# Hymba block with a hierarchical mixture of experts: routing by token halves, column-wise down weights in whole loads, and an interleaved scatter

## The chip, the core and the metric

The kernel runs on one core of one Trainium2 chip. The metric is the device time of one execution in microseconds (us); lower is better. All data are float32. The five engines are called PE (TensorE), DVE (VectorE), ACT (ScalarE), POOL (GpSimd) and SP (SyncE, which here only issues DMAs).

## What is computed

One block over 256 tokens of width 1024: a mixer (RG-LRU beside causal attention), a cross attention to 256 memory rows, and a mixture of experts, each on a normed input and added to the residual, then a last norm. The change lies at the seam between the cross attention and the experts, and at the end:

```python
h = h + memory_cross_attention(rms_norm(h, norm_cross), mem, ...)      # ends with o @ w_xo
h = h + hier_moe(rms_norm(h, norm_ffn), ...)
return rms_norm(h, norm_final)

# hier_moe, for each token
g_logits = xt @ w_router_group + b_router_group            # 4 groups, the best one is taken
e_logits = xt @ w_router_expert + b_router_expert          # 32 experts, 8 a group, two are taken
gates = g_w * top_p / sum(top_p)
# for each expert, over its tokens
gate, up = split(x @ w_gate_up[e])                         # 1024 x 1024
y = (silu(gate) * up) @ w_down[e]                          # 512 x 1024
out[token] += gate_weight * y
```

All 32 experts are read whatever the routing is: 32 x 6.29 MB (gate/up 4.19 MB, down 2.10 MB).

## The kernel before, in words

The program is one block with an instruction list per engine, ordered by hand; engines meet only at semaphores. PSUM has eight banks; `JOBS` (a table at the top) is the order of their fills, and `begin`, `end`, `release`, `await_fill` and `await_read` turn it into waits. SBUF holds a `ring` of 12 units of 16 KB a partition (2.10 MB each); each of the four experts in flight has three units (`EXPERT_UNITS`): gate/up part 0, gate/up part 1 (contraction rows 0 to 511 and 512 to 1023), and down. Before the experts, parts of the ring serve as landing, split and work buffers of the dense stages.

**Dense stages.** Weights come in 30 halves of 1 MB (`load_half`), are split into a high and a low part by ACT (`split_hi`) and by DVE or POOL (`split_lo`; POOL has halves 6, 8, 10, 12, L1126), and each product is three float32r matmuls (`channels`, L561; `tokens`, L575). A weight half's landing slot and split slot come free at the end of its last use (`LAST_JOB`, `half_used`), and SP's prefetch of expert weights into ring units that are still in use waits for these events (`load_expert`, L442). The last three units of the first four experts wait for half 28 (unit 3), and for the end of job `xo3` (units 4 and 5).

**The seam.** The last projection is four jobs: xo0 and xo1 are columns 0 to 511 of token halves 0 and 1, xo2 and xo3 columns 512 to 1023. DVE adds each to `res` (L1435). PE then transposes `res` (`turn("Tf")`, L544), ACT and DVE copy it with the norm's gain (L899, L1440), PE multiplies by the router (`route`, L758), and `open_sum` (L740) puts `res` into the four accumulator banks with an identity matmul. ACT sums squares (L914), DVE and POOL make 1/rms (L1188, L1120). DVE takes the logits (L1455), finds the best group and two best experts by a chain of small steps (`first_of_max`, L1477 to L1507) for both token halves at once, PE counts ranks (L774 to L776), DVE finds slots (`take_slots`, L1522, L1527), POOL and PE prepare an overflow count. An expert has 32 slots.

**The expert loop.** `Fori` over 8 groups of four experts. PE gathers the group's tokens with one-hot matmuls (L794, 16 matmuls of two records each), DVE writes xg (L1552). For each expert PE does two gate/up parts (L811, 16 matmuls each in four column strips, `gu_used` counts halves of a part), ACT and DVE form silu(gate) * up (L1084, L1562, L1564), PE transposes it (L828), ACT copies it (L899), PE does the down product (L836: 4 k-tiles x 4 strips of 256 columns, strip s holding output columns 256 s to 256 s + 255), and ACT and DVE copy two strips each into `ybuf` (L899, L1568). After the fourth expert PE scatters with four 128x512 matmuls (L845) onto the accumulators. A product of float32 takes two records in the profile. SP refills: gate/up parts at L447 (`load_part`, 16 KB a partition in one load) as `gu_used` allows, down in two loads of 1 MB at L442, each 8 KB a partition, as `y_done` allows.

**The end.** SP loads `norm_final` (0.5 MB, L507) behind the last weights. After the last scatter, for each token half: ACT squares 1024 columns with a sum (L1110), DVE makes the mean (L1188), POOL the power (L1120), DVE scales by it and by the gain (L1613, two of 512 columns), SP stores (L522). Ahead of that every engine loads a flag and branches on it (`value_load`, `If`): the overflow path is not taken.

## Time and profile before

| | |
|---|---|
| device time, median of 3 (lowest, highest) | 672.67 us (672.4, 674.99) |
| the profiled execution: own time, span | 671.75 us, 670.0 us |
| busy: PE, DVE, ACT, POOL | 510.9, 220.9, 168.9, 41.0 us |
| moved by DMA | 237.85 MB, mean 355 GB/s |
| mean granted clock of PE | 0.922 of full |

The span runs from the first to the last recorded event of the execution; the own time also holds what lies around it (1.8 us). All starts below are us from the beginning of the span. A stretch of the granted clock at 1.00 is PE at 2.4 GHz, one at 0.50 is PE at 1.2 GHz. In rows of the timeline, instructions of one line are merged: start, duration from first start to last end, and how many (x); brackets hold the idle time before and what ended it.

### The profile page before, as it was taken

To read this page: it belongs to the slowest core of one execution; us is meant where nothing else is said; L and a number is where in the kernel's file an instruction comes from. 1 tells how busy PE (TensorE), PEld (TensorE's weight loads), DVE (VectorE), ACT (ScalarE), POOL (GpSimd) and SP (SyncE) were. 2 spreads that over 40 slices of the span, in tenths; PEclk is the share of its full clock that TensorE was granted. 3 is DMA by queue.
4 is the path that set the end of the run, shared out by engine and by line. 5 is a ranking of instruction groups with operands and counts; after the bars stand their busy time and mean duration, and the time that the engine had idled before them with its cause. 6 is when DMAs were issued, how large, how long until landed. Compare 5 with 4: busy or idle time off the path is not lost.

```text
span 670.0 us, 11410 instructions
## 1 busy us (share of the span) xinstructions
PE 510.9 (76%) x4768; PEld 351.9 (53%) x4768; DVE 220.9 (33%) x425; ACT 168.9 (25%) x325; POOL 41.0 (6%) x25
## 2 busy tenths in 40 slices
PE   3999999999999987978656756855684585657544
PEld 3988998789888654545223423422352252224221
...
GB/s 345 285 194 183 314 127 142 138 398 248 186 282 382 357 238 425 425 430 427 427 426 427 422 425 426 429 427 426 427 426 424 423 429 427 427 426 427 423 425 156
DMA packets 25637, 237.85 MB, mean 355 GB/s; under 512 B 2832, under 2 KB 2960, under 8 KB 4368
## 3 DMA queue, kind: packets, MB, share of 16 engines
...
q8 instruction: 15, 0.25, 0.1%
q14 instruction: 6, 0.05, 0.0%
HBM read 236.49 MB, written 1.05 MB: 355 GB/s over the span
## 4 chain that ended last, share of the span: by engine, by line
SPq 48%; PE 38%; DMA 7%; issue 3%; DVE 2%; ACT 1%; POOL 1%; DVEq 0%; POOLq 0%
SPq L447 30%; SPq L442 18%; PE psum L575 14%; PE psum L561 11%; DMA ring<-in_w_down 5%; PE psum L811 3%; PE psum L836 2%; DMA landing<-in_dense 1%; PE psum L794 1%; PE psum L544 1%; PE psum L709 1%; PE psum L732 1%; PE psum L845 1%; PE psum L758 1%; POOL stat L1120 1%
## 5 line engine op out<-in xcount | busy, mean ns | idle before, releaser
L811 PE MATMUL psum<-ring,xg 128*32 128x256 f32 x2048 | 152.6, 454 | 87.4 <-DMA ring<-in_w_gate_up 87.4
L811 PEld LDWEIGHTS psum<-ring,xg 128*32 128x32 f32 x2048 | 78.8, 126 | 154.6 <-issue 129.7
L575 PE MATMUL psum<-split_w,split_act 128*128 128x512 f32 x432 | 101.8, 393 | 1.2 <-DVE res L1379 1.2
L575 PEld LDWEIGHTS psum<-split_w,split_act 128*128 128x128 f32 x432 | 80.4, 188 | 18.3 <-DVE res L1379 1.7
L1562 DVE SCALAR_TENSOR_TENSOR small<-small,psum 128x128 f32<-128x128 f32 x32 | 9.2, 288 | 214.8 <-ACT small L1084 214.8
L1084 ACT ACTIVATE small<-psum 128x128 f32<-128x128 f32 x32 | 8.9, 277 | 279.3 <-PE psum L811 279.3
L836 PE MATMUL psum<-ring,small 128*32 128x256 f32 x1024 | 67.2, 400 | 12.9 <-ACT small L899 11.7
L561 PE MATMUL psum<-split_act,split_w 128*128 128x256 f32 x576 | 72.2, 289 | 0.9 <-DVE split_act L1208 0.9
L561 PEld LDWEIGHTS psum<-split_act,split_w 128*128 128x128 f32 x576 | 71.6, 197 | 1.7 <-DVE split_w L1229 1.2
L899 ACT ACTIVATE split_w<-landing 128x2048 fp32r<-128x2048 f32 x30 | 57.4, 1915 | 51.2 <-PE psum L575 27.6
L1195 DVE TENSOR_TENSOR split_w<-landing,split_w 128x2048 fp32r<-128x2048 f32 x25 | 58.9, 2361 | 30.6 <-ACT split_w L899 30.6
L1568 DVE COPY ybuf<-psum 32x256 f32<-32x256 f32 x64 | 27.2, 424 | 95.3 <-PE psum L836 94.8
L836 PEld LDWEIGHTS psum<-ring,small 128*32 128x32 f32 x1024 | 30.2, 113 | 40.0 <-ACT small L899 18.1
L899 ACT ACTIVATE ybuf<-psum 32x256 f32<-32x256 f32 x64 | 23.9, 373 | 72.5 <-PE psum L836 72.2
L1120 POOL TENSOR_TENSOR stat<-stat,ctab 128x2 f32<-128x2 f32 (+2 forms) x7 | 6.9, 991 | 546.6 <-DVE stat L1188 536.6
L845 PE MATMUL psum<-ybuf,small 128*128 128x512 f32 x64 | 29.4, 602 | 8.6 <-DVE ybuf L1568 8.6
L828 PE MATMUL psum<-ctab,small 128*128 128x128 f32 x32 | 10.8, 338 | 30.2 <-DVE small L1564 30.2
L794 PEld LDWEIGHTS psum<-ntake,res 128*128 128x128 f32 x256 | 29.8, 192 | 3.3 <-issue 3.3
L794 PE MATMUL psum<-ntake,res 128*128 128x128 f32 x256 | 29.9, 275 | 0.0
L828 PEld LDWEIGHTS psum<-ctab,small 128*128 128x128 f32 x32 | 4.5, 141 | 47.1 <-DVE small L1564 47.1
L1552 DVE TENSOR_TENSOR xg<-psum,ctab 128x512 f32<-128x512 f32 x16 | 11.1, 691 | 44.5 <-PE psum L794 44.5
L845 PEld LDWEIGHTS psum<-ybuf,small 128*128 128x128 f32 x64 | 11.5, 189 | 23.7 <-ACT ybuf L899 12.3
...
## 6 DMA issues: line engine op xcount, KB each, us to landing
...
```

Of the source, the lines that this page charges most:

```text
L442: sp.dma_start(unit(u)[:, n], src).then_inc(loaded[u][side], 16)
L447: sp.dma_start(unit(u), w_gate_up[e, part]).then_inc(loaded[u][1], 16)
L561: i = mm(b[:, 256 * c:256 * c + 256], w[a][:, k, P * c:P * c + P], src[t][:, k, :], start=k == 0 and n == 0, stop=k == KC - 1 and n == 2)
L575: i = mm(b, src[t][:, k0 + k, P * h:P * h + P], w[a][:, k, :], start=first and k == 0 and n == 0, stop=last and k == CT - 1 and n == 2)
L794: i = mm(bank(GATHER + part)[:, P * k:P * k + P], res[:, h, P * c:P * c + P], ntake[:, h], start=h == 0, stop=h == NH - 1)
L811: i = mm(half[SLOTS * strip:SLOTS * strip + SLOTS], xg[:, CT * part + k, SLOTS * j:SLOTS * j + SLOTS], w[:, k, :, P * strip:P * strip + P] ...
L828: tr(bank(HY)[:, 256:256 + P], hid, ident).then_inc(hid_turned, 1)
L836: i = mm(bank(HY)[SLOTS * strip:SLOTS * strip + SLOTS, 0:256], hidT[:, SLOTS * k:SLOTS * k + SLOTS], w[:, k, 256 * strip:256 * strip + 256 ...
L845: i = mm(bank(ACC_BANKS[2 * h + cb]), give[:, P * h:P * h + P], ybuf[:, 512 * cb:512 * cb + 512], start=False, stop=True, skip_group_check ...
L899: return nc.scalar.activation(dst, src, ACT.Identity, scale=scale, bias=bias)
L1195: V.tensor_tensor(lo, raw(m, chunks_of(m)), hi.bitcast(F32), ALU.subtract).then_inc(w_lo, 1)
L1568: i = V.tensor_copy(ybuf[SLOTS * j:SLOTS * j + SLOTS, 256 * strip:256 * strip + 256], bank(6)[r, 0:256])
```

## The change

- **Routing by token halves.** The last projection does token half 0 over weight halves 28 and 29, then half 0 is turned, routed and chosen, and half 1 of the projection runs behind that; logits, choice, rank and slots are computed for one half at a time (`choose`, `place`, `find_slots`). Squares are summed in four pieces of 512 columns into PSUM. The logits move to another part of `small`.
- **Overflow flag.** It is worked out from the number of tokens of each expert, by two matmuls and three DVE steps ahead of the loop, without POOL.
- **POOL's splits** wait for DVE's convolution (`conv_done`).
- **Down weights** are laid out by output columns (side 0 is 0 to 511, side 1 is 512 to 1023), and loaded as one 2 MB load of 16 KB a partition; for the last expert alone, part 1 and down come in two halves. The down product runs side by side: 2 sides x 4 k-tiles x 4 strips of 128 columns, sides in banks 6 and 4, copied to `ybuf` side by side.
- **Gather** of part 1 is cut: two of four tiles before the first gate/up part, two behind it.
- **Scatter.** Columns 0 to 511 of token half 0 are scattered after side 0 of the fourth expert, the other three behind side 1. The last group is unrolled out of the loop on PE and SP.
- **Norm gain** is loaded after routing into its own buffer (shared with the router's table), ahead of the first refill.
- **Last norm.** Four squares of 512 columns; DVE multiplies by the gain before 1/rms is known, then ACT (columns 0 to 511) and DVE (the rest) scale.

```diff
-    down = np.asarray(inputs["w_down"])[0].reshape(EXPERTS, 2, 2, P, D).transpose(0, 1, 3, 2, 4)
+    down = np.asarray(inputs["w_down"])[0].reshape(EXPERTS, CT, P, 2, 512).transpose(0, 2, 3, 1, 4)
     return {"in_w_gate_up": np.ascontiguousarray(gate_up).reshape(EXPERTS, 2, P, UNIT),
-            "in_w_down": np.ascontiguousarray(down).reshape(EXPERTS, 2, P, HALF)}
+            "in_w_down": np.ascontiguousarray(down).reshape(EXPERTS, P, UNIT)}
...
-        latetab = sb("latetab", [P, (KC + 1) * N_ROUTES])
+        after_routing = sb("after_routing", [P, D])
+        latetab = after_routing[:, 0:(KC + 1) * N_ROUTES]
...
-                    src = w_gate_up[e, part, :, n] if part < 2 else w_down[e, side]
+                    src = (w_gate_up[e, part] if part < 2 else w_down[e])[:, n]
                     sp.dma_start(unit(u)[:, n], src).then_inc(loaded[u][side], 16)
 
             def load_part(e, j, part):
 
                 u = EXPERT_UNITS[j][part]
-                sp.dma_start(unit(u), w_gate_up[e, part]).then_inc(loaded[u][1], 16)
+                src = w_gate_up[e, part] if part < 2 else w_down[e]
+                sp.dma_start(unit(u), src).then_inc(loaded[u][1], 16)
...
+            for h in range(NH):
+                await_read(sp, f"route{h}")
+            sp.dma_start(gain_final, norm_final.partition_broadcast(P)).then_inc(gain_loaded, 16)
+            def refill(g, last):
+
                 for j in range(BATCH):
                     for part in range(2):
                         sp.wait_ge(gu_used, 4 * BATCH * g + (4 * (j - BATCH) + 2 * part + 2))
-                        load_part(BATCH * g + j, j, part)
-                    sp.wait_ge(y_done, BATCH * g + (j + 1 - BATCH))
-                    load_expert(BATCH * g + j, j, 2)
-            sp.wait_ge(gu_used, 4 * (EXPERTS - BATCH + 1))
-            sp.dma_start(gain_final, norm_final.partition_broadcast(P)).then_inc(gain_loaded, 16)
+                        if last and j == BATCH - 1 and part:
+                            load_expert(BATCH * g + j, j, part)
+                        else:
+                            load_part(BATCH * g + j, j, part)
+                    if last and j == BATCH - 1:
+                        for side in range(2):
+                            sp.wait_ge(y_done, 2 * BATCH * g + (2 * (j - BATCH) + side + 1))
+                            load_expert(BATCH * g + j, j, 2, (side,))
+                    else:
+                        sp.wait_ge(y_done, 2 * BATCH * g + (2 * (j - BATCH) + 2))
+                        load_part(BATCH * g + j, j, 2)
+
+            with sp.Fori(1, BATCHES - 1) as g:
+                refill(g, False)
+            refill(BATCHES - 1, True)
...
             tokens_whole(26, ["xo0", "xo1"], ys_, "xpv")
-            tokens(28, ["xo2", "xo3"], ys_, 0, last=False)
+            tokens(28, ["xo2", "xo3"], ys_, 0, last=False, halves=(0,))
+            tokens(29, ["xo2", "xo3"], ys_, CT, first=False, halves=(0,))
             for c in (0, 1):
                 await_read(pe, f"xo{c}")
             turn("Tf", res, (0, 1))
-            tokens(29, ["xo2", "xo3"], ys_, CT, first=False)
-
-
...
             pe.wait_ge(router_loaded, 16)
-            route(0)
-            for c in (2, 3):
-                await_read(pe, f"xo{c}")
-            turn("Tf", res, (2, 3))
-            route(1)
-            open_sum(0)
-
+            for c in (0, 1):
+                await_read(pe, f"Tf{c}")
+            route(0, 0)
+            route(1, 0)
+            await_read(pe, "Tf2")
+            route(0, 1)
+            tokens(28, ["xo2", "xo3"], ys_, 0, last=False, halves=(1,))
+            tokens(29, ["xo2", "xo3"], ys_, CT, first=False, halves=(1,))
+
+            picked = rt(4)
             pe.wait_ge(chosen, 1)
-            picked = rt(4)
-            b = begin("rank")
-            mm(b[:, 0:EXPERTS], const("before"), picked[:, 0], start=True, stop=True)
-            mm(b[:, EXPERTS:2 * EXPERTS], const("before"), picked[:, 1], start=True, stop=False)
-            end(mm(b[:, EXPERTS:2 * EXPERTS], ones, picked[:, 0], start=False, stop=True), "rank")
-            open_sum(1)
+            end(mm(begin("rank0")[:, 0:EXPERTS], const("before"), picked[:, 0], start=True, stop=True), "rank0")
+            open_sum(0, 0)
+            await_read(pe, "xo3")
+            turn_late("Tf3", 1, (4, 5))
+            turn_late("Tf4", 1, (6, 7))
+            open_sum(1, 0)
+            for c in (3, 4):
+                await_read(pe, f"Tf{c}")
+            route(1, 1)
+            begin("rank1")
+            mm(pb("rank1")[:, 0:EXPERTS], ones, picked[:, 0], start=True, stop=False)
+            pe.wait_ge(late_sumsq, 2 * NH)
+            open_sum(0, 1)
+            open_sum(1, 1)
+            pe.wait_ge(chosen, 2)
+            end(mm(pb("rank1")[:, 0:EXPERTS], const("before"), picked[:, 1], start=False, stop=True), "rank1")
             GATHER, HY, GU = 4, 6, 7
             for h in range(NH):
                 await_read(pe, f"route{h}")
-            await_read(pe, "rank")
-
-            pe.wait_ge(over_ready, 1)
+                await_read(pe, f"rank{h}")
+            picked_all = rt(4)
             begin("over")
-            end(mm(pb("over")[:, OVER:OVER + NH * EXPERTS], ones, rt(12).rearrange("p h e -> p (h e)"), start=True,
-                   stop=True), "over")
-            with pe.Fori(0, BATCHES) as g:
+            for h in range(NH):
+                i = mm(pb("over")[:, OVER:OVER + EXPERTS], ones, picked_all[:, h], start=h == 0, stop=h == NH - 1)
+            end(i, "over")
...
+            def scatter(g, cb, halves):
+
+                pe.wait_ge(y_act, 2 * BATCH * g + (2 * BATCH + cb - 1))
+                pe.wait_ge(y_dve, 2 * BATCH * g + (2 * BATCH + cb - 1))
+                for h in halves:
+                    mm(bank(ACC_BANKS[2 * h + cb]), give[:, P * h:P * h + P], ybuf[:, 512 * cb:512 * cb + 512],
+                       start=False, stop=True, skip_group_check=True).then_inc(scattered, 1)
+
+            def group(g, last):
+
 
                 pe.wait_ge(taken, g + 1)
-                for part in range(2):
-                    for k in range(CT):
+                def gather(part, ks):
+
+                    for k in ks:
                         for h in range(NH):
                             c = CT * part + k
                             i = mm(bank(GATHER + part)[:, P * k:P * k + P], res[:, h, P * c:P * c + P],
                                    ntake[:, h], start=h == 0, stop=h == NH - 1)
-                    i.then_inc(gathered, 1)
+                    if ks[-1] == CT - 1:
+                        i.then_inc(gathered, 1)
+
+                gather(0, range(CT))
+                gather(1, range(2))
...
+                            if part:
+                                gather(1, range(2, CT))
                             pe.wait_ge(xg_ready, 2 * g + (1 + part))
...
+                    for side in range(2):
+                        if last and j == BATCH - 1:
+                            pe.wait_ge(loaded[u][side], (32, 16 * BATCHES)[side])
+                        elif side == 0:
+                            pe.wait_ge(loaded[u][0], 16)
+                            pe.wait_ge(loaded[u][1], 16 * g + 16)
+                        for k in range(CT):
+                            for strip in range(BATCH):
+                                i = mm(bank((HY, GATHER)[side])[SLOTS * strip:SLOTS * strip + SLOTS, 0:P],
+                                       hidT[:, SLOTS * k:SLOTS * k + SLOTS], w[:, side, k, P * strip:P * strip + P],
+                                       start=k == 0, stop=k == CT - 1, tile_position=(0, SLOTS * strip))
+                        i.then_inc(y_done, 1)
+                        if j == BATCH - 1:
+                            scatter(g, 0, (side,))
+                scatter(g, 1, range(NH))
+
+            with pe.Fori(0, BATCHES - 1) as g:
+                group(g, False)
+            group(BATCHES - 1, True)
...
+            late_squares(0, 0)
             turned_tokens(0)
-            for h in range(NH):
-                await_read(act, f"xo{2 + h}")
-                sum_squares(res, 4, (h,))
-            turned_tokens(2)
-            act.wait_ge(group_arg, 1)
+            late_squares(1, 0)
+            late_squares(0, 1)
+            late_squares(1, 1)
...
-            for h in range(NH):
-                act.wait_ge(scattered, NH * (BATCHES - 1) + h + 1)
-                nc.scalar.activation(final_squares.rearrange("p (c n) -> p c n", c=2), psum[:, 2 * h:2 * h + 2, :], ACT.Square,
-                                     accum_out=stat[:, SS + FINAL + h:SS + FINAL + h + 1]).then_inc(final_sq, 1)
-                act.wait_ge(final_sq, h + 1)
+            for cb in range(2):
+                for h in range(NH):
+                    act.wait_ge(scattered, 2 * NH * (BATCHES - 1) + 2 * cb + h + 1)
+                    col = SS + FINAL + 2 * cb + h
+                    nc.scalar.activation(final_squares[:, 0:512], bank(ACC_BANKS[2 * h + cb]), ACT.Square,
+                                         accum_out=stat[:, col:col + 1]).then_inc(final_sq, 1)
+                    act.wait_ge(final_sq, 2 * cb + h + 1)
+            for h in range(NH):
+                act.wait_ge(final_gain, h + 1)
+                act.wait_ge(final_rstd, h + 1)
+                copy(fin[:, h, 0:512], fin[:, h, 0:512], stat[:, RS + FINAL + h:RS + FINAL + h + 1]).then_inc(final_act, 1)
...
+            pool.wait_ge(conv_done, 1)
             split_lo(6)
...
+            for h in range(NH):
+                pool.wait_ge(meansq, 4 + h)
+                power(6 + h, 1, rstd)
...
+            choose(0)
+            add_xo("xo3", 1, 1)
+            late_tokens("Tf4", 6, 2, 1)
+            late_mean(1)
+            place(0)
+            link(find_slots(0, 0))
+            slots_times_rstd(0)
+            choose(1)
+            place(1)
+            find_slots(1, 0).then_inc(slots_found, 1)
+            dve.wait_ge(slots_found, 1)
+            slots_times_rstd(1).then_inc(taken, 1)
...
+            await_fill(dve, "over")
+            link(V.tensor_reduce(soft[:, 0:1], pb("over")[:, OVER:OVER + EXPERTS], AX.X, ALU.max))
+            link(V.tensor_scalar(soft[:, 0:1], soft[:, 0:1], SLOTS + 0.5, None, ALU.is_ge))
+            release(V.tensor_copy(flag, soft[:, 0:1]), "over")
+            await_read(dve, "over")
...
+            def times_gain(h, cb):
+                n = slice(512 * cb, 512 * cb + 512)
+                return V.tensor_tensor(fin[:, h, n], bank(ACC_BANKS[2 * h + cb]), gain_final[:, n], ALU.mult)
+
             for h in range(NH):
                 dve.wait_ge(final_sq, h + 1)
-                mean(FINAL + h, 1, D).then_inc(final_ms, 1)
+                times_gain(h, 0).then_inc(final_gain, 1)
+            link(mean(FINAL, NH, D))
+            for h in range(NH):
+                dve.wait_ge(final_sq, 3 + h)
+                col = MS + FINAL + h
+                V.scalar_tensor_tensor(stat[:, col:col + 1], stat[:, SS + FINAL + 2 + h:SS + FINAL + 3 + h], 1.0 / D,
+                                       stat[:, col:col + 1], ALU.mult, ALU.add).then_inc(final_ms, 1)
+                times_gain(h, 1).then_inc(final_gain, 1)
+            for h in range(NH):
+                dve.wait_ge(final_gain, NH + h + 1)
                 dve.wait_ge(final_rstd, h + 1)
-                for cb in range(2):
-                    n = slice(512 * cb, 512 * cb + 512)
-                    V.scalar_tensor_tensor(fin[:, h, n], bank(ACC_BANKS[2 * h + cb]),
-                                           stat[:, RS + FINAL + h:RS + FINAL + h + 1], gain_final[:, n],
-                                           ALU.mult, ALU.mult).then_inc(final_out, 1)
+                V.tensor_scalar(fin[:, h, 512:], fin[:, h, 512:], stat[:, RS + FINAL + h:RS + FINAL + h + 1], None,
+                                ALU.mult).then_inc(final_dve, 1)
...
```

## Rows read from the trace of the kernel before

**Rows 1.** The page, 40 slices of 16.75 us: GB/s moved by DMA

```profile
GB/s 345 285 194 183 314 127 142 138 398 248 186 282 382 357 238 425 425 430 427 427 426 427 422 425 426 429 427 426 427 426 424 423 429 427 427 426 427 423 425 156
```

**Rows 2.** The page, chain that ended last, share of the span by engine

```profile
SPq 48%; PE 38%; DMA 7%; issue 3%; DVE 2%; ACT 1%; POOL 1%; DVEq 0%; POOLq 0%
```

**Rows 3.** Windows: us, busy of PE, PEld, DVE, ACT, POOL, granted clock, DMA share, GB/s

```profile
233.00:241.00 8.00, 8.00 (x94) 6.04 (x96) 5.17 (x21) 0.00 (x0) 0.47 (x1) 1.00 0.10 39
241.00:243.00 2.00, 1.33 (x19) 0.53 (x11) 0.57 (x2) 0.66 (x2) 0.00 (x0) 1.00 0.92 221
...
250.00:640.00 390.00, 262.66 (x3107) 141.22 (x3107) 60.01 (x170) 40.09 (x122) 0.00 (x0) 0.88 1.01 426
224.00:231.00 7.00, 6.89 (x20) 4.59 (x20) 3.23 (x21) 0.21 (x1) 0.70 (x1) 0.51 1.00 378
```

**Rows 4.** Timeline of SP's DMA issues before the expert stream

```profile
214.12 0.80 SPq L442 DMA_DIRECT2D ring<-in_w_gate_up  x2
...
220.47 0.80 SPq L442 DMA_DIRECT2D ring<-in_w_gate_up  x2
...
240.24 2.05 SPq L447 DMA_DIRECT2D ring<-in_w_gate_up  x2
```

**Rows 5.** Timeline of PE at the seam

```profile
214.72 5.72 PE L575 MATMUL psum<-split_w,split_act 128*128 128x512 f32 x24
...
220.28 1.87 PE L758 MATMUL psum<-latetab,xg 128*128 128x36 f32 x16
...
224.11 3.60 PE L758 MATMUL psum<-latetab,ybuf 128*128 128x36 f32 x16 [1.06 <-DVE ybuf L1440]
...
234.32 3.65 PEld L794 LDWEIGHTS psum<-ntake,res 128*128 128x128 f32 x32
```

**Rows 6.** Timeline of DVE at the seam

```profile
220.48 0.69 DVE L1435 TENSOR_TENSOR res<-psum,res 128x512 f32<-128x512 f32 x1 [2.03 <-PE psum L575]
...
228.12 0.29 DVE L1477 TENSOR_REDUCE soft<-small 128x8 f32<-128x64 f32 x2
...
231.44 0.22 DVE L1507 TENSOR_TENSOR small<-small 128x64 f32<-128x64 f32 x1
...
233.74 0.48 DVE L1527 TENSOR_SCALAR ntake<-small,stat 128x128 f32<-128x128 f32 x2
...
236.52 0.68 DVE L1552 TENSOR_TENSOR xg<-psum,ctab 128x512 f32<-128x512 f32 x1
```

**Rows 7.** Timeline of PE in the last group, gate/up products released by landings

```profile
623.36 3.62 PE L811 MATMUL psum<-ring,xg 128*32 128x256 f32 x32 [2.97 <-DMA ring<-in_w_gate_up]
...
633.23 3.26 PE L811 MATMUL psum<-ring,xg 128*32 128x256 f32 x32 [2.60 <-DMA ring<-in_w_gate_up]
638.13 1.93 PE L811 MATMUL psum<-ring,xg 128*32 128x256 f32 x32 [1.65 <-DMA ring<-in_w_gate_up]
```

**Rows 8.** Timeline of the end of the span (and one down product of an earlier expert)

```profile
628.70 1.93 PE L836 MATMUL psum<-ring,small 128*32 128x256 f32 x32 [0.37 <-ACT small L899]
...
657.75 0.59 PEld L836 LDWEIGHTS psum<-ring,small 128*32 128x32 f32 x16 [0.61 <-DMA ring<-in_w_down]
658.89 0.76 ACT L899 ACTIVATE ybuf<-psum 32x256 f32<-32x256 f32 x2 [2.40 <-PE psum L836]
...
659.91 3.67 PE L845 MATMUL psum<-ybuf,small 128*128 128x512 f32 x8 [1.08 <-DVE ybuf L1568]
...
663.68 1.02 ACT L1110 ACTIVATE ring<-psum 128x1024 f32<-128x1024 f32 x1 [0.66 <-PE psum L845]
...
664.60 0.19 ACT L1110 ACTIVATION_READ_ACCUMULATOR ring<-psum 128x1 f32 x1
...
666.10 1.41 DVE L1613 SCALAR_TENSOR_TENSOR ring<-psum,stat,ring 128x512 f32<-128x512 f32 x2 [0.67 <-POOL stat L1120]
```

**Rows 9.** Timeline of DVE's convolution and POOL's first split behind it

```profile
36.71 5.09 DVE L1273 SCALAR_TENSOR_TENSOR work<-work,ctab 128x256 f32<-128x256 f32 x12
...
43.00 5.49 POOL L1126 TENSOR_TENSOR split_w<-landing,split_w 128x2048 fp32r<-128x2048 f32 x1 [18.53 <-ACT split_w L899]
```

252 lines of the change are left out of this document (134 added, 118 removed).

## The prediction

> **What bounds the kernel now.** I read the page's slices first. From slice 15 on the DMA engines move 422 to 430 GB/s in every slice until the last one, while before it they are often half idle [rows 1]. The chain of waits says the same: 48% of the span is the DMA queue's own issuing, which stands blocked behind transfers in flight [rows 2]. The windows by stage then give the sizes: 426 GB/s at a DMA share of 1.01 over the 390 us from 250 to 640, with PE busy two thirds of that time, DVE 60 us and ACT 40 us [rows 3]. So the expert stage is a stream of bytes: 28 experts x 6.29 MB remain to be loaded after the ring of four experts is full, 176 MB at 426 GB/s = 413 us, and nothing that compute does within it matters. The time is: when that stream starts, its rate, and what follows its last byte.
>
> **Its start.** The windows show 39 GB/s in 233 to 241: the ring is full and nothing may be loaded until the first expert's first half of gate/up weights has been used. That is the issue at 240.24 [rows 4]; with the thin 241 to 243 (221 GB/s) behind it [rows 3] the stream has an effective start of 242.0 (0.44 MB by 243). The path to 240.24 by engine: PE's last output projection ends near 220.44, DVE adds xo3 at 220.48, the route parts follow, then 3.5 us of choosing (228.12 to 231.66, both token halves together), the gather from 234.38 and half a gate/up product behind it [rows 5, 6]. Within it the granted clock fell to 0.5 of full (0.51 over 224 to 231 [rows 3]), and as many records of routing took 3.60 us instead of 1.87 [rows 5].
>
> **Its end.** The last half of down weights lands at 657.75, the span ends at 669.96: a tail of 12.2 us [rows 8].
>
> **The change part by part.** All times are on the scale of the profiled execution (span 669.96, own time 671.75, which is 0.9 below the median of 672.67).
>
> *GpSimd's split behind the convolution.* The added wait is for DVE's convolution, whose last operations run from 36.71 for 5.09 us, to 41.80; GpSimd's first such split starts at 43.00 today, released by ACT [rows 9]. The wait is met before it is reached: 0. What queues behind it on GpSimd starts no later.
>
> *Routing by halves.* PE now does token half 0 of the last projection first (24 of the 48 matmuls), then turns and routes half 0, then does half 1. 24 of its matmuls take 5.6 us (5.72 for a stretch with its hand-over [rows 5]). Half 0 is done at 213.9, the turns (8+4 transposes of 128x128, 0.12 each) by 215.5, the three route parts (24 records at 0.117 [rows 5], after DVE's copies) by about 218.9, half 1 (24 matmuls) by 224.4: xo3 comes 3.9 us later than today. Choosing one half lies between 1.8 us (half of 3.54) and 3.5; most of a step is fixed cost, so I take 3.2. For half 0 it lies under the half-1 matmuls and costs nothing; uncovered it would cost those 3.2 us. After 224.4 on the path: rank0 0.3, open_sum 0.92 (four matmuls of 512 columns in 3.67 [rows 8]), turns 0.5, open_sum 0.92, route 0.95, some 0.4 of hand-overs = 228.4; logits and 3.2 us of choosing, to 232.0; rank, place and slots of one half 1.5, to 233.5. So the slots are there 0.7 us before today's 234.22 (233.74 + 0.48 [rows 6]), although two choices are now made instead of one.
>
> *Gather split, overflow flag ahead of the loop.* Only 24 of 32 gather records (0.115 each [rows 5]) stand ahead of the first gate/up half, so PE could begin at 236.4. But DVE's xg is late next: today it ends at 237.20, 3.0 us after the slots (gates, gtake, xg [rows 6]), and the flag's three new steps with their waits, 0.25 each, go in between. xg: 233.5 + 3.0 + 0.75 = 237.3; product 1.93 [rows 7]; first refill issued at 239.4 instead of 240.24. **Gain 0.8**, which would be 1.5 without the flag. The flag's matmuls lie in PE's wait: 0.
>
> *What that hands to the queue.* SP's loads of the last three prefetch units hang on the projection: one at 214.12 (after weight half 28), two from 220.47 (after xo3) [rows 4]. In the new order half 28 is free only after its second use, at 221.7, and xo3 at 224.5. Counted back from 233.5, the last two units ran from 222.4 (9.8 us and 1.3 lost) and the one before from about 216.3 or 216.5, so the load before that ends near 216.3. There the queue now runs dry; it idles to about 223.2, then needs 3 x 4.9 = 14.7 us, to 238 or 239, where now it was done at 233.5. The norm gain, 0.5 MB or 1.2 us, is moved from behind the last weights, where it was free, to just there. So the queue comes dry at 239 to 240, right when the first refill is issued. The idle time is moved, not removed: 8 us of it lay at 233 to 242, now 7 lie at 216 to 223. An even faster route would bring little. Effective start 241.2 instead of 242.0: **-0.8**, between -2.5 (queue never dry again) and +5 (rival C).
>
> *Down weights in 2 MB loads.* A row of a partition becomes 16 KB instead of 8. The matmuls that wait for landings give the price: from gate/up part 1 of one expert to part 0 of the next (a down unit in halves and a gate/up unit) 623.36 to 633.23 = 9.87, then one gate/up unit 633.23 to 638.13 = 4.90 [rows 7]. Down costs 4.97 where gate/up costs 4.90. For the 27 units still to come that are merged: 27 x 0.07 = 1.9; the last expert's part 1 is now split (+0.1), and an unrolled last group means more instructions to fetch (+0.1). **-1.7**, between 0 (the differences are one hundredth of a reading) and -2.7 (0.1 each). What the loads' own start costs is weighed under rival D.
>
> *Narrow down products.* 16 matmuls of 256 columns become 32 of 128: 32 records in 1.93 us [rows 8] become 64. If streaming stays the limit it is still 1.9 us; if each record keeps its 0.06 us, 3.9. I take 1.9: four strips run side by side and 128x128 records come at 0.114 each when alone. Either way PE waits for weights in the stream (it is busy two thirds of it), so the price there is 0; in the tail it is 0 to 1.8.
>
> *Tail.* Today, after 657.75 (16 of the down product's 32 records are left, 1.0 us): copies to 659.7, four scatter matmuls 3.67, square and read-out until 664.8, mean and power to 666.10, two products of 0.7, the store from 667.5 to 669.96 [rows 8]. New: columns 0 to 511 are done and scattered for half 0 before the last megabyte lands (that scatter ends at about 658.1, 0.4 late; if that overlap fails it is the 0.92 of the matmul); side 1 takes 0.9, copies 0.6 (0.76 at twice the width), ACT's load of the flag 0.5 (its price is not shown: it lies today between 659.7 and the first square, two squares of 1.02 and their gap before 664.8, so 0 to 2.2; I take the low part, being one word), four squares of about 0.87 (half of 1.02, read-out 0.19, hand-over) to 663.8, where ACT and no longer PE's 2.8 us of scatter ends last. Power until 665.1, DVE's last gain product and two scalings (0.7 + 2 x 0.4) to 666.1 instead of 667.5. **-1.4**, between -2.5 and +0.5.
>
> Sum: -0.8 - 1.7 - 1.4 = **-3.9**: own time 667.9, and against the median 672.67 - 3.9 = **668.8**.
>
> **The rivals.** About 0.5% (3.4 us) is what a measurement of this kernel can tell from no change.
>
> *B, the clock falls under the early route.* From 213.9 to 218.9 PE now does only transposes, 36-column products and waits, as it does today from 220.4 to 224.1, after which the clock was 0.51 over 224 to 231. Then part of half 1's matmuls run at half speed: the rows price it at 1.7 (3.60 - 1.87), more if longer; xo3 moves to 226.3 or later, first refill to 241.1, effective start 242.9: the first term becomes +0.9 and the time 670.5. For it: the stretch is as thin and longer than today's. Against: dense matmuls follow at once. Chance 0.33. The Trainium skill's page TensorE: Matmul & The Clock Gate, section HAM oscillation, says that PE waiting between bursts falls back to the low clock; the trace's clock row agrees.
>
> *C, slower: the clock is low from xo3 through the first group.* While half 1 is chosen PE has nothing (about 230.4 to 232.1) and then only small products. If the clock is at half from 224.4 on, route and sums add 3.0, the gather 2.7, the first gate/up product 1.3 (3.26 against 1.93 [rows 7]): from an issue at 239.4 to one at 246.4 at most; part of the gather lies beside DVE's 0.9, so 245.5. The stream starts at 247 instead of 242, +5.0 - 3.1 = +1.9: 674.6. It decides once the low clock covers the gather; without that it is rival B. Chance 0.06.
>
> *D, every load has a start of its own.* After the idle stretch the first bytes came about 1.1 us after the issue at 240.24 [rows 3, 4]. If each of the 27 merged loads saved that, 30 us would go: 638. Against it stands 426 GB/s at share 1.01 with halves and whole loads mixed in the queue: the start is hidden in the queue. Chance 0.01. The Trainium skill's page DMA: Bandwidth & Descriptors, section Bandwidth, gives 341 GB/s for single 1 MB transfers and 425 for 16 MB and asks for large ones; by its figures merging would bring about 1.3 us each, an estimate of 36 us. The trace disagrees for loads that are queued.
>
> *E, the change does not do what it says in the tail.* Narrow products at 0.06 a record and ACT's flag load late: the tail brings 0, 670.2. Chance 0.12.
>
> **How the numbers follow.** Forecast case 0.48, 665.6 to 670.0 by its own bounds; B 0.33, E 0.12, C 0.06, D 0.01. Faster by over 0.5% (below 669.3) is four fifths of the forecast case, a third of B, a quarter of E and D: 0.53. Slower by over 0.5%: 0.05 (C where the packets bring nothing as well, and B where the low clock lasts). Within: 0.42. The range, 665.2 to 671.9, holds the forecast case and most of B and E.
>
> **What would show it.** Right: DMA near zero at 217 to 223 and almost none at 235 to 240; xo3's add near 224.6; issue of the first refill near 239.4; landings 4.90 apart for all three units of an expert; last landing to end of span about 10.8. Wrong: a gap in the DMA just before the first refill, PEclk 0.5 after 216 or in the gather, a rate that stays 426, or a tail of 12. I would be most wrong if the late prefetch loads push the stream's start past 242.

## The result, and the profile after

Changed kernel 666.59 us (665.56 to 669.61, 6 runs), kernel before 672.6 us (671.19 to 678.04, 6 runs) on the same chip: ratio 0.989, 95% interval [0.9858, 0.9922]. The number came out inside the range that was predicted (668.8, range 665.2 to 671.9), and faster by over 0.5%, which was given 0.53. A later measurement of the same kernel (e6, 12 runs, below) gave 0.9939 [0.9908, 0.9969]. Medians and ranges here are of all executions, while the ratios leave out those over 1.5% above the fastest of their kernel: one of e4's, and four of the kernel before beside e1 to e8. The profiled execution has a span of 664.3 and a time of its own of 666.09, where before had 669.96 and 671.75: 5.7 us less.

The page of the changed kernel, slices and chain by engine (against [rows 1, 2]), and its loads of whole units (kind and count, KB each, median us from issue to landing):

```profile
GB/s 357 283 199 177 318 135 178 131 403 230 190 279 356 296 374 428 431 427 427 427 427 431 427 431 427 428 427 427 430 428 431 428 427 427 427 431 429 427 419 148
...
PE 44%; DMA 38%; SPq 11%; DVE 3%; ACT 1%; issue 1%; POOL 1%; ACTq 0%; DVEq 0%
...
ring<-in_w_gate_up SPq DMA_DIRECT2D x55, 2048.0 KB, 49.3
ring<-in_w_down SPq DMA_DIRECT2D x27, 2048.0 KB, 49.4
```

Its windows, columns as in rows 3:

```profile
216.00:223.00 7.00, 7.00 (x34) 5.37 (x34) 3.78 (x22) 0.20 (x1) 0.00 (x0) 1.00 0.38 128
232.00:235.00 3.00, 3.00 (x18) 2.78 (x21) 1.61 (x7) 0.00 (x0) 0.00 (x0) 0.50 1.02 423
233.00:239.00 6.00, 5.22 (x54) 3.69 (x56) 2.04 (x6) 0.00 (x0) 0.00 (x0) 0.82 0.89 322
250.00:640.00 390.00, 270.57 (x4063) 172.41 (x4057) 69.70 (x230) 49.72 (x181) 0.00 (x0) 0.87 1.01 428
```

And its timeline, from the first product to the stores:

```profile
13.62 11.87 PE L579 MATMUL psum<-split_act,split_w 128*128 128x256 f32 x96 [0.86 <-DVE split_act L1287]
...
36.02 5.09 DVE L1352 SCALAR_TENSOR_TENSOR work<-work,ctab 128x256 f32<-128x256 f32 x12
...
41.19 6.61 POOL L1205 TENSOR_TENSOR split_w<-landing,split_w 128x2048 fp32r<-128x2048 f32 x1 [17.40 <-DVE work L1352]
...
206.07 0.69 DVE L1513 TENSOR_TENSOR res<-psum,res 128x512 f32<-128x512 f32 x1 [0.53 <-PE psum L593]
...
230.50 4.43 PE L839 MATMUL psum<-ntake,res 128*128 128x128 f32 x24
...
237.11 4.13 SPq L453 DMA_DIRECT2D ring<-in_w_gate_up  x2
...
628.61 1.93 PE L865 MATMUL psum<-ring,xg 128*32 128x256 f32 x32 [1.69 <-DMA ring<-in_w_gate_up]
633.50 2.76 PE L865 MATMUL psum<-ring,xg 128*32 128x256 f32 x32 [2.95 <-DMA ring<-in_w_gate_up]
...
638.39 3.34 PE L894 MATMUL psum<-ring,small 128*32 128x128 f32 x64 [0.58 <-DMA ring<-in_w_down]
...
643.29 1.93 PE L865 MATMUL psum<-ring,xg 128*32 128x256 f32 x32 [1.56 <-DMA ring<-in_w_gate_up]
...
648.18 1.07 PE L865 MATMUL psum<-ring,xg 128*32 128x256 f32 x16 [1.42 <-DMA ring<-in_w_gate_up]
...
651.05 1.08 PE L894 MATMUL psum<-ring,small 128*32 128x128 f32 x32 [0.37 <-ACT small L956]
...
652.94 1.10 PE L827 MATMUL psum<-ybuf,small 128*128 128x512 f32 x2 [0.81 <-DVE ybuf L1691]
653.97 1.08 PE L894 MATMUL psum<-ring,small 128*32 128x128 f32 x32
654.98 2.84 PE L827 MATMUL psum<-ybuf,small 128*128 128x512 f32 x6
...
659.84 1.81 SPq L540 DMA_DIRECT2D out<-ring  x4
```

What to see. The queue runs dry at 216 to 223 (128 GB/s) and is busy at 233 to 239 (322 GB/s), the reverse of [rows 3]: the idle time was moved, as forecast. Landings, read from the products that they release, are 4.89 to 4.90 apart for all three units of an expert (628.61, 633.50, 638.39, 643.29), where down took 4.97. But the largest piece lies where I had put zero: the add of xo1, which comes ahead of everything that the change does to the routing, is at 206.07 instead of 208.68. Cut at three points, the 5.7 us are: start to that add -2.61; add to first refill 31.04 instead of 31.56, -0.52; first refill to the last gate/up landing 411.07 instead of 412.65 (652.89 - 240.24 in the trace of before), -1.58; that landing to the end 16.12 instead of 17.07, -0.95.

### The profile page after: what moved, and what is told of

Same layout as the page of the kernel before. It is cut to its first block, busy times and chain, and to the rows that moved or that the text cites. A ratio compares the mean times of both kernels' runs of the same rounds, so it can differ in the third digit from the quotient of the medians.

```text
span 664.3 us, 13610 instructions
## 1 busy us (share of the span) xinstructions
PE 515.4 (78%) x5794; PEld 381.9 (57%) x5794; DVE 236.3 (36%) x518; ACT 181.3 (27%) x399; POOL 42.0 (6%) x25
## 4 chain that ended last, share of the span: by engine, by line
PE 44%; DMA 38%; SPq 11%; DVE 3%; ACT 1%; issue 1%; POOL 1%; ACTq 0%; DVEq 0%
DMA ring<-in_w_gate_up 29%; PE psum L593 15%; SPq L453 11%; PE psum L579 10%; DMA ring<-in_w_down 8%; PE psum L865 6%; PE psum L894 3%; PE psum L839 2%; PE psum L827 2%; DMA landing<-in_dense 1%; PE psum L750 1%; PE psum L727 1%; PE psum L562 1%; SPq L447 1%; PE psum L771 1%
## 5 line engine op out<-in xcount | busy, mean ns | idle before, releaser
L865 PE MATMUL psum<-ring,xg 128*32 128x256 f32 x2048 | 139.6, 420 | 66.0 <-DMA ring<-in_w_gate_up 59.7
L865 PEld LDWEIGHTS psum<-ring,xg 128*32 128x32 f32 x2048 | 73.5, 118 | 119.1 <-issue 82.5
L894 PE MATMUL psum<-ring,small 128*32 128x128 f32 x2048 | 80.7, 319 | 23.7 <-DMA ring<-in_w_down 16.0
L894 PEld LDWEIGHTS psum<-ring,small 128*32 128x32 f32 x2048 | 67.6, 128 | 40.3 <-issue 26.8
L1691 DVE COPY ybuf<-psum 32x128 f32<-32x128 f32 x128 | 37.2, 291 | 121.9 <-PE psum L894 121.1
L956 ACT ACTIVATE ybuf<-psum 32x128 f32<-32x128 f32 x128 | 34.2, 267 | 99.0 <-PE psum L894 98.3
L1199 POOL TENSOR_TENSOR stat<-stat,ctab 128x1 f32<-128x1 f32 (+2 forms) x8 | 7.3, 912 | 550.7 <-DVE stat L1737 433.6
L827 PE MATMUL psum<-ybuf,small 128*128 128x512 f32 x64 | 37.0, 704 | 6.5 <-DVE ybuf L1691 6.5
L839 PE MATMUL psum<-ntake,res 128*128 128x128 f32 x256 | 33.6, 287 | 0.1
L1205 POOL TENSOR_TENSOR split_w<-landing,split_w 128x2048 fp32r<-128x2048 f32 x4 | 21.4, 5338 | 30.6 <-DVE work L1352 17.4
```

The lines of the kernel that those rows point to most:

```text
L827: mm(bank(ACC_BANKS[2 * h + cb]), give[:, P * h:P * h + P], ybuf[:, 512 * cb:512 * cb + 512], start=False, stop=True, skip_group_check=Tru ...
L839: i = mm(bank(GATHER + part)[:, P * k:P * k + P], res[:, h, P * c:P * c + P], ntake[:, h], start=h == 0, stop=h == NH - 1)
L865: i = mm(half[SLOTS * strip:SLOTS * strip + SLOTS], xg[:, CT * part + k, SLOTS * j:SLOTS * j + SLOTS], w[:, k, :, P * strip:P * strip + P] ...
L894: i = mm(bank((HY, GATHER)[side])[SLOTS * strip:SLOTS * strip + SLOTS, 0:P], hidT[:, SLOTS * k:SLOTS * k + SLOTS], w[:, side, k, P * strip ...
L956: return nc.scalar.activation(dst, src, ACT.Identity, scale=scale, bias=bias)
L1205: nc.gpsimd.tensor_tensor(lo, raw(m, chunks_of(m)), hi.bitcast(F32), ALU.subtract).then_inc(w_lo_pool, 1)
```

## The experiments

The same cuts for every profiled execution (us). "First product" and "convolution" are the durations of the lines of 13.62 and 36.02 above. "To first refill" is from xo1's add to the issue of the first refill, "to last gate/up landing" from there to the start of the product that the last gate/up weights release (in e11 and e12, where idle products stand before it, to the landing itself), and "to end" from there to the end of the span.

| kernel | first product | convolution | xo1 add at | to first refill | to last gate/up landing | to end | span |
|---|---|---|---|---|---|---|---|
| before | 13.93 | 5.09 | 208.68 | 31.56 | 412.65 | 17.1 | 670.0 |
| after | 11.87 | 5.09 | 206.07 | 31.04 | 411.07 | 16.1 | 664.3 |
| e1 before again | 11.87 | 9.42 | 213.07 | 29.91 | 412.54 | 19.5 | 675.0 |
| e2 before, whole down | 13.44 | 5.09 | 207.72 | 33.27 | 410.53 | 19.4 | 670.9 |
| e3 after, half down | 13.25 | 5.09 | 207.91 | 31.09 | 412.4 | 16.8 | 668.2 |
| e4 after, no wait | 11.86 | 9.48 | 212.31 | 35.48 | 410.43 | 16.2 | 674.4 |
| e5 before, wait | 11.88 | 5.09 | 206.38 | 29.91 | 412.56 | 17.1 | 665.9 |
| e6 after again | 13.2 | 5.09 | 207.89 | 31.08 | 410.29 | 18.6 | 667.9 |
| e7 after, old seam | 13.52 | 5.09 | 207.43 | 30.94 | 410.52 | 19.7 | 668.6 |
| e8 after, scatters late | 13.91 | 5.09 | 208.69 | 31.05 | 410.54 | 17.0 | 667.3 |
| e9 before, wait, whole down | 11.88 | 5.09 | 206.12 | 31.58 | 410.37 | 18.2 | 666.3 |
| e10 after, gather filled | 11.89 | 5.09 | 207.05 | 32.61 | 410.46 | 17.7 | 667.8 |
| e11 after, tail filled | 13.74 | 5.1 | 208.15 | 31.07 | 410.4 | 16.5 | 666.1 |
| e12 after, both filled, scatters and gain late | 13.22 | 5.09 | 207.45 | 31.02 | 410.6 | 16.8 | 665.9 |

### e1, e4, e5: GpSimd's wait

e1 is the kernel before, unchanged, beside e2 to e4. e4 takes the wait out of the changed kernel, e5 puts it, and nothing else, into the kernel before:

```diff
 e4
-            pool.wait_ge(conv_done, 1)
             split_lo(6)
 ...
 e5
+            pool.wait_ge(conv_done, 1)
             split_lo(6)
 ...
```

> The kernel before, unchanged, for a second profile of it. Theory A (the start of the span differs by chance): the first product of 96 matmuls, 13.93 us in the profile of before and 11.87 in that of after, takes another value here, anywhere from 11.8 to 14, according to when the granted clock rises, so that the seam may start up to 2.6 us earlier without any change. Rival B (the change itself made the start quicker): it is again close to 13.9, and the end of job xo1 again near 208.7. Both: last landing to end of span 12.2 us, rate 426 GB/s, ratio 1.00.

> The changed kernel without GpSimd's wait for the convolution. My step said that the wait costs and brings nothing, as it is met before it is reached. In the profile of after the split starts at 41.19 on the wait's release, 1.0 us after ACT had its part ready. Theory A: gain and loss within 0.2 us at the end of the first gate product and at xo1. Rival B (GpSimd beside the convolution slows DVE, and the wait brings the 2 us of the start): convolution's last 12 steps take over 5.5 us instead of 5.09, and xo1 ends 2 us later.

> The kernel before with one line more: GpSimd waits for the end of the convolution ahead of its first split of weights in that stage; nothing else of the change. Theory (the stalled step): where TensorE's clock rises early, so that the first product takes 11.87 us, the split of the kernel before begins at about 40.6 us beside the convolution, and one step of VectorE stands for 4.8 us; with the wait the convolution takes 5.1 us in every execution, the split begins at 41.2 at the earliest, and about half of the executions get 3 to 4.5 us shorter. The median falls by 1.5 to 3.5 us (ratio 0.995 to 0.998), the slowest executions fall to about 674 and the fastest stay as they are. Rival (the wait is worth nothing, as I predicted, and the early stages of the changed kernel were shorter by the clock's chance alone): ratio 1.000 within 0.002, with the same spread of 671 to 682, and a convolution of over 9 us in a profile whose first product takes 11.87.

Measured: e1 675.33 us (670.96 to 678.88), ratio 0.9995 [0.9963, 1.0027]. e4 672.48 (667.62 to 678.13), 0.9948 [0.9912, 0.9984]. e5 669.89 (667.37 to 675.39), 0.9929 [0.9896, 0.9961], beside a before of 673.5. One line of the change, alone, makes the kernel 3.6 us faster by the medians (2.6 to 7.0 by the interval of the ratio): nearly as much as the whole change beside it (e6, 669.67). Taking the line out of the changed kernel shows less clearly what it is worth: e4's ratio of 0.9948 stands against 0.989 and 0.9939 with the line, and the intervals overlap.

The timelines show how. The first product in the profile of before, and then e1, where it is shorter:

```profile
14.30 13.93 PE L561 MATMUL psum<-split_act,split_w 128*128 128x256 f32 x96 [0.88 <-DVE split_act L1208]
```

```profile
13.92 11.87 PE L561 MATMUL psum<-split_act,split_w 128*128 128x256 f32 x96 [1.27 <-DVE split_act L1208]
...
36.31 9.42 DVE L1273 SCALAR_TENSOR_TENSOR work<-work,ctab 128x256 f32<-128x256 f32 x12
...
40.55 4.89 POOL L1126 TENSOR_TENSOR split_w<-landing,split_w 128x2048 fp32r<-128x2048 f32 x1 [16.46 <-ACT split_w L899]
...
47.99 2.50 PE L575 MATMUL psum<-split_w,split_act 128*128 128x512 f32 x5 [4.09 <-DVE split_w L1195]
```

The convolution's twelve steps in e1 (durations in ns, minimum, median, maximum; first and last start):

```profile
L1273 DVE SCALAR_TENSOR_TENSOR work<-work,ctab x12: 480/481/4808, 36.3 to 40.9; 128x256 f32<-128x256 f32 x12
```

Eleven steps take 0.48 us; one, beside GpSimd's split of 4.89 us, takes 4.81. PE then waits 4.1 us for DVE's own split behind it, and the add of xo1 comes at 213.07. Whether the two meet hangs on the first product. Where it takes 11.87, ACT is ready with its part at 40.5 to 40.8 and lets GpSimd go while DVE still convolves, which would last until 41.4 to 41.6. Where it takes 13.2 to 13.9, that hand-over comes at 41.8 to 43.0, behind the convolution, as in [rows 9] and e2, which have no wait either. e5 with a short first product:

```profile
36.39 5.09 DVE L1274 SCALAR_TENSOR_TENSOR work<-work,ctab 128x256 f32<-128x256 f32 x12
...
41.56 6.61 POOL L1126 TENSOR_TENSOR split_w<-landing,split_w 128x2048 fp32r<-128x2048 f32 x1 [17.39 <-DVE work L1274]
...
206.38 0.69 DVE L1436 TENSOR_TENSOR res<-psum,res 128x512 f32<-128x512 f32 x1 [0.54 <-PE psum L575]
...
236.29 2.06 SPq L447 DMA_DIRECT2D ring<-in_w_gate_up  x2
```

Among the short starts the two without the wait (e1, e4) add xo1 at 213.07 and 212.31, the four with it (after, e5, e9, e10) at 206.07 to 207.05: 6 to 7 us each time. The long starts lie at 207.4 to 208.7 with or without it. So in these profiles the wait doesn't give 6 us to all executions; it turns the worst case into the best one. Six of fourteen profiles had the short start; 6/14 of 6.5 us is 2.8, an estimate near the 3.6.

The Trainium skill, page SBUF — State Buffer, section Who interferes with whom, says that a VectorE instruction with two inputs in SBUF contends with a GpSimd instruction that reads SBUF, and that the loser is blocked for the whole of the other's instruction. The trace agrees: 4.81 us beside 4.89, in place of 0.48. The other way round fits too: above, GpSimd's split at 41.19 takes 6.61, where others take 4.58 to 4.60. DVE's split (41.03, 2.29 us) came first and ended at 43.32, and from there to the end of GpSimd's at 47.80 are 4.48 us; there nobody waits for it.

Why the first product has two lengths isn't settled. In the windows from 14 to 20, before got through 29 of its records and e1 through 50 (0.20 and 0.12 us each), while the column of the granted clock stands at 1.00 in both.

### e2, e3: the down weights' rows

e2 gives the kernel before 16 KB rows and one 2 MB load per down unit; e3 takes the merging back in the changed kernel's loop:

```diff
 e2 (np.asarray(inputs["w_down"])[0] is left out of the first two lines)
-    down = ....reshape(EXPERTS, 2, 2, P, D).transpose(0, 1, 3, 2, 4)
+    down = ....reshape(EXPERTS, CT, P, D).transpose(0, 2, 1, 3)
...
-                    load_expert(BATCH * g + j, j, 2)
+                    load_part(BATCH * g + j, j, 2)
...
 e3
-                        load_part(BATCH * g + j, j, 2)
+                        load_expert(BATCH * g + j, j, 2)
...
```

> The kernel before with down weights in rows of 16 KB and one 2 MB load for each refill, nothing else. If bytes in packets of 8 KB are slower by the 0.07 us for 2 MB that the landings showed: 28 x 0.07 = 1.9 us off the stream, 428 GB/s instead of 426 in 250 to 640, landings 4.90 apart, span about 668 where nothing else differs, ratio 0.997. Rival (the 2 MB loads bring nothing, the gain is the seam and the tail): rate stays at 426, ratio 1.000. Rival (each load has a start of its own): 30 us less.

> The changed kernel with the down refills in two loads of 1 MB of 8 KB rows again (the columns stay by sides, the product waits for each side alone). If the rows of 16 KB are what made the stream faster: rate back to 426 in 250 to 640, down units 4.97 instead of 4.90, span longer by 1.8 to 2.6 us. Rival (the rate came from fewer waits of the queue, not from packets): rate stays 428.

Measured: e2 672.65 us (669.31 to 678.08), 0.997 [0.9934, 1.0006]; e3 670.11 (668.57 to 672.77), 0.9931 [0.9904, 0.9957]. The medians alone don't settle 2 us in a kernel that spreads over 8. The stream does: first refill to last gate/up landing is 412.4 to 412.7 in the four executions with 8 KB rows (before, e1, e3, e5) and 410.3 to 411.1 in the ten others of the table, whatever else they do. The rate from 250 to 640 is 426 GB/s with the halves and 428 or 429 without. Merging is worth 2.0 us of the stream. e3's landing is read from this row of weight loads, since its products ran on at the low clock past it:

```profile
651.41 0.45 PEld L865 LDWEIGHTS psum<-ring,xg 128*32 128x32 f32 x8 [0.41 <-DMA ring<-in_w_gate_up]
```

What in the merging does it isn't separated: both runs change the length of the rows and the number of loads together. By their pages e2 moved the same bytes as before in 21605 packets instead of 25637, which is 144 fewer for each of the 28 merged pairs, and 16 of these 144 are packets under 512 bytes (2384 in all instead of 2832).

### e6, e7, e8: routing by halves, and the scatter between the sides

e6 is the changed kernel again. e7 gives it back the routing of both halves together. e8 moves the scatter:

```diff
 e8
                         i.then_inc(y_done, 1)
-                        if j == BATCH - 1:
-                            scatter(g, 0, (side,))
+                scatter(g, 0, range(NH))
                 scatter(g, 1, range(NH))
```

> The changed kernel unchanged, as the measure for the two runs beside it. If the stalled step explains its narrow spread: 665.5 to 670, median 666.5 to 668.5, and a profile with a convolution of 5.1 us. If that was luck of its six executions: some at 671 or over, and a convolution of over 9 us where the first product takes 11.87.

> The changed kernel with the routing of before: both token halves together (adds, turns, logits, choice, ranks, slots), all else of the change kept, the slots of the gather ahead of the loop among it. Theory: the split of the gather stays, so the first refill is issued about 0.5 us later than in the changed kernel measured from the add that opens the stage (31.5 in place of 31.0), and the kernel is 0.3 to 0.8 us slower than the changed kernel in the same job. Rival (the halves gain more than that, since they keep TensorE busy through the routing and so hold its clock up): the windows of the route show 0.5 to 0.8 of the clock and the kernel is 1.5 us or more slower. Rival (the halves bring nothing): the same within 0.2 us.

> The changed kernel with all four scatter products of the last two experts behind both sides of the last down product, as one block, in place of one scatter between the sides. In the changed kernel's trace the product of side 1 (653.97) waited 1.0 us behind a scatter that waited for its rows, with its weights long there. Theory: side 1 follows side 0 at once and ends 0.75 to 1.0 us earlier, its copies with it, and the last scatter, which then carries one product more (0.55 us), ends 0.2 to 0.7 us earlier; last landing to end shrinks by that, and the kernel is 0.2 to 0.7 us faster than the changed kernel. Rival (the change's own reason, that the early scatter takes work off the end): 0.3 to 0.6 us slower, since one scatter of 0.55 to 0.6 us comes behind the last copy.

Measured: e6 669.67 us (667.75 to 671.67), 0.9939 [0.9908, 0.9969]; e7 670.95 (665.03 to 672.98), 0.9938 [0.9905, 0.9972]; e8 668.31 (666.67 to 669.05, 6 runs), 0.9901 [0.9862, 0.9939]. e6 lies 1 to 2 us above my expectation, and three of its runs are at 671 or over (671.08, 671.3, 671.67), which I had named as the sign that the first six executions were low by luck; its profile had a long first product, so it doesn't test the stalled step. e7's ratio is e6's, though its median is 1.3 us higher and its runs spread over 8 us, where e6's spread over 4. The table shows e7's first refill no later (30.94) than with the halves (31.04 to 31.09). So the theory's 0.5 us isn't seen, but intervals of 0.3% either way can't exclude it. e6, its timeline and two windows:

```profile
232.32 4.57 PE L839 MATMUL psum<-ntake,res 128*128 128x128 f32 x24
...
238.97 4.14 SPq L453 DMA_DIRECT2D ring<-in_w_gate_up  x2
...
649.26 1.07 PE L865 MATMUL psum<-ring,xg 128*32 128x256 f32 x16 [1.42 <-DMA ring<-in_w_gate_up]
...
652.20 1.79 PE L894 MATMUL psum<-ring,small 128*32 128x128 f32 x32 [0.43 <-ACT small L956]
...
656.74 1.94 PE L894 MATMUL psum<-ring,small 128*32 128x128 f32 x32
```

```profile
232.00:235.00 3.00, 2.94 (x16) 2.83 (x16) 2.35 (x14) 0.00 (x0) 0.00 (x0) 0.60 1.03 434
653.00:659.00 6.00, 5.21 (x55) 2.80 (x48) 0.84 (x3) 0.78 (x3) 0.00 (x0) 0.50 0.04 15
```

Two things are to be read here. The gather of 24 records takes 4.57 us, with the granted clock at 0.50 for a part of it. That is so in all of after, e3, e6, e8 and e11 (4.43 to 4.58, mean granted clock 0.62 to 0.64 over the gather). In the kernel before 32 records took 3.79 in four profiles of five (before, e1, e5, e9, at 1.00; 4.64 in e2), and with the old routing in the changed kernel (e7) 24 took 2.92, at 1.00. And in the tail the clock is at the 1.2 GHz level in e6 and e7, and the down products of 32 records take 1.8 to 1.9 us each; in after and e4 it is at 2.4 and they take 1.08. Between landing and end these profiles are 2.5 to 3.6 us apart (16.1 against 18.6 and 19.7).

e8, whose clock was low for part of the tail:

```profile
650.28 1.56 PE L865 MATMUL psum<-ring,xg 128*32 128x256 f32 x16 [1.42 <-DMA ring<-in_w_gate_up]
...
653.76 3.64 PE L894 MATMUL psum<-ring,small 128*32 128x128 f32 x64 [0.37 <-ACT small L955]
...
657.33 3.79 PE L827 MATMUL psum<-ybuf,small 128*128 128x512 f32 x8
```

It ended 17.0 us after the landing, 1.6 sooner than e6. With both sides in one block there is no second wait for copies (0.81 in the timeline of after) and no scatter at half speed ahead of the last weights' product. That the scatter between the sides, which the change added for the tail, costs time where the clock is low is an argument from these two profiles, and the clock came back at different times in them; the intervals of e6 and e8 overlap. Where the clock is high, e12 ends its scatters no sooner than after.

### e9: two parts of the change alone

The kernel before with the edits of e2 and e5.

> The kernel before with two parts of the change alone: GpSimd's wait behind the convolution, and the down weights in one 2 MB load of 16 KB rows each. No routing by halves, no split gather, no narrow down products, no scatter between the sides, gain still last in the queue. Theory (the wait is worth 2 to 3.6 us in the median, the rows 2.0 us of stream, and the rest of the change next to nothing on average): ratio 0.989 to 0.993, level with the whole change; from the first refill's issue to the last gate/up landing 410.5 us in place of 412.6. Rival (the rest of the change brings 1.5 us or more, by slots, split gather and tail, as I predicted 2.2 of it): ratio 0.994 or above, and over 1.5 us behind the changed kernel (0.989 and 0.994 in its two measurements).

Measured: 669.95 us (667.0 to 675.7), 0.9941 [0.9907, 0.9974], beside a before of 674.84. By the ratio it falls to the rival by a hair; the interval holds both. It is level with the changed kernel's second measurement and 0.005 behind its first. Its stream is as expected, 410.37. Nine of its twelve runs lie between 667.0 and 670.6 and three between 674.8 and 675.7, a group that e6's twelve runs don't have; no profile fell in it, so its cause is open.

### e10, e11, e12: keeping TensorE busy

e10 runs three products of 512 columns, read by nobody, ahead of the wait for the second choice; e11 runs such products in the last expert's waits; e12 is both, with e8's scatters and the gain vector's load moved behind the last weights.

```diff
 e10
+            for _ in range(3):
+                mm(bank(4), ident, res[:, 0, 0:512], start=True, stop=True, skip_group_check=True)
             pe.wait_ge(chosen, 2)
 e11 (keep_busy(n): n such products into bank 5; last expert only)
+                                    keep_busy(2)    # ahead of its part 0, and of the second half of part 1
+                        keep_busy(1)
                     pe.wait_ge(hid_ready, n)
```

> The changed kernel with three idle products of 512 columns, whose result nobody reads, on TensorE ahead of its wait for the second half's choice, where it stood for 1.55 us. In all four profiles of the changed kernel with a fast start, TensorE stands there and the granted clock is 0.50 in the middle of the gather right behind, whose 24 products take 4.4 to 4.6 us. Theory (the standing time takes the clock down): with the gap filled the gather's 24 products take 2.8 to 3.2 us at a clock of 1.00, and the first refill is issued 29.5 to 30.0 us behind the add that opens the stage in place of 31.05; the time falls by less than that, 0.5 to 1.2 us, since the queue's prefetch is still moving until about 31.5 us behind that add. Rival (the clock falls on its own schedule): the gather still 4.4 to 4.6, the time the same. Rival on the slow side: the idle products end late and hold up the rank, 0.5 slower.

> The changed kernel with idle products of 512 columns in the waits of the last expert alone: two ahead of its first gate/up weights, two ahead of the second half of part 1, one ahead of the hidden units. Of five profiles with this tail, two (the changed kernel's own and the one without GpSimd's wait) ended 16.1 to 16.2 us after the last product of gate/up began and two (the changed kernel again, and with the old routing) 18.6 and 19.7, with down products of 32 records at 1.8 to 1.9 us in place of 1.08. Theory (the clock falls in these waits, in some executions): with the waits filled the tail takes 16.1 to 16.4 in the profile and the median falls by 1 to 2 us, with a narrower spread. Rival (the clock's level in the tail is set by the stream before, not by these waits): the same median and spread as the changed kernel. Rival on the slow side: where the clock is low anyway, the idle products take 1 us each and the time rises by up to 1 us.

> All that helped or should help, on the changed kernel: the idle products of both runs beside it, all four scatters behind the last down product, and the gain vector's load at the end of the queue. Sum of the parts against the changed kernel: gather and gain together 1.5 to 2.5 us (the refill issued 1 to 1.5 earlier, and 1.2 us of gain load out of its way), the tail 1 to 2 us by the clock and 0.7 by the scatters: 3 to 5 us, so a ratio of 0.983 to 0.988 against the kernel before, and a profile with a span of 661 to 664. Rival (gather and gain bring nothing, since the refill's start is set elsewhere): 1.5 to 2.5 us, ratio 0.987 to 0.991.

Measured: e10 669.08 us (665.41 to 671.37), 0.9913 [0.988, 0.9947]; e11 667.61 (666.13 to 668.67), 0.9893 [0.986, 0.9926]; e12 667.92 (666.41 to 669.36), 0.9903 [0.9869, 0.9936]. e12, timeline and the window of its gather:

```profile
232.65 2.94 PE L845 MATMUL psum<-ntake,res 128*128 128x128 f32 x24
...
236.33 1.93 PE L874 MATMUL psum<-ring,xg 128*32 128x256 f32 x32 [0.73 <-DVE xg L1683]
...
238.47 4.14 SPq L453 DMA_DIRECT2D ring<-in_w_gate_up  x2
...
649.51 1.07 PE L874 MATMUL psum<-ring,xg 128*32 128x256 f32 x16
...
652.32 1.08 PE L905 MATMUL psum<-ring,small 128*32 128x128 f32 x32 [0.37 <-ACT small L966]
...
654.07 1.08 PE L905 MATMUL psum<-ring,small 128*32 128x128 f32 x32 [0.67 <-DMA ring<-in_w_down]
655.08 3.70 PE L829 MATMUL psum<-ybuf,small 128*128 128x512 f32 x8
```

```profile
232.00:235.00 3.00, 2.94 (x25) 2.83 (x26) 2.42 (x13) 0.00 (x0) 0.00 (x0) 1.00 1.01 426
```

The theory of the gather holds: TensorE's standing still took the clock down, and filled waits hold it at 1.00 (2.94 us, not 4.4 to 4.6). Still the first refill came 31.02 behind the add (238.47 - 207.45), and in e10, whose early route was slow as well (0.76 over 216 to 223), 32.6. The three idle products took 2.74 us in a gap of 1.55, so the rank, which ran 0.06 us behind the second choice in after, ran 0.9 behind it; and PE, whose gather ends sooner, now waits 0.73 for DVE ahead of the first gate/up product. What the clock gave, the late rank and DVE took.

In the tail the down products of e11 and e12 all took 1.08. With the waits filled that is two profiles of two, and without, three of seven (after, e3, e4), so it fits the theory and doesn't show it.

e12's sum of 3 to 5 us isn't there, and not even 1: the refill wasn't earlier, the gain load was out of its way already (410.29 to 410.54 in e4, e6, e7 and e8 with it in place), and the last product at full clock waits for its own weights (0.67) when no scatter stands before it, so the block of four scatters ends at 658.8, 9.7 behind the landing (649.1, which is 2.5 after that of the first half), just as in after (657.8, 9.6). From there e12 took 0.6 us more to the end than after did: its four stores were issued over 2.99 us instead of 1.81, for a reason that the profile doesn't give. e8, e11 and e12 can't be told from the changed kernel by these intervals. Their six runs each lie within 2.4 to 3.0 us, against 4 in both measurements of the changed kernel; e8 has this without any idle product, so the idle products aren't shown to be what narrows the spread.

## Why the prediction was right, and where it was not

**GpSimd's wait, "The wait is met before it is reached: 0": this step failed.** It is worth 3.6 us by e5 (2.6 to 7.0), the largest single part. I argued from one execution, in which the split came 1.2 us after the convolution [rows 9], and took a gap that depends on ACT's hand-over for a fixed one. The right question was what happens where the split comes 1.2 us earlier: one step of the convolution stands for 4.8 us in place of 0.48 (e1, e4).

**Down weights, -1.7, range 0 to -2.7: right**, -2.0 across fourteen profiles. Down units land as fast as gate/up units, which is how it was priced; whether the longer rows do it or the fewer loads isn't separated.

**Routing and split gather, -0.8: mis-sized, next to nothing.** The predicted length was good: 30.7 from the add to the first refill, and 31.04 to 31.09 measured. The base was not: 31.56 was one draw of a kernel that shows 29.91 twice, 31.58 and 33.27 (e1, e5; e9; e2). 1.7 us of it were the low clock over 224 to 231 that I read in [rows 3, 5] and then took for part of the kernel.

Against the average of the five, 31.25, the five undisturbed profiles of the changed route (after, e3, e6, e8, e11) gain 0.2; with e4 beside them they lose 0.6, and the two best of the old route (29.91) are 1.1 ahead of all of them. Rival B (low clock under the early route) occurred in e4 (35.48, granted clock 0.50 from 222 to 225) and mildly in e10 (32.61); in the five others the clock fell later, in the gather, a small form of rival C without its price: the first refill came 0.4 behind the forecast's 30.7, and the queue was still moving 421 to 434 GB/s from 232 to 235.

The Trainium skill, page TensorE: Matmul & The Clock Gate, section HAM oscillation, has TensorE fall back to the low clock when it waits between bursts; here that bore on the gather and the tail more than on the early route.

**The queue's dry spell: right**, 216 to 223, moved and not removed. The sign "almost none at 235 to 240" wasn't met: after moved 269 GB/s there, and ran dry only from 237 to 238 (74 GB/s), just ahead of the first bytes of the refill.

**Tail, -1.4: -0.95**, where the clock is high (16.1 against 17.1). The overlap failed in the way priced at 0.9: side 1's product stood 1.0 us behind the scatter that waited for copies. Narrow products were right: 64 records in 1.95 us, 32 in 1.08. I didn't see that the tail's clock has two levels worth 2.5 us.

**The sum.** -3.9 predicted; -6.0 by medians, then -3.8. The terms as measured (3.6, 2.0, 0.2, 0.95) make 6.8, more than either, and e9 with 5.6 of them gained 4.9. So that the sum came out is in part luck: a term of 3.6 stood at zero, and the parts don't all add up. What stays open is that remainder of 1 to 3 us. The start, the gather and the tail shift single profiles by 1 to 4 us each, and medians over 6 to 12 runs can hold different shares of them; that this makes the remainder is a guess that no run tests.
